# Gate weights kept in SBUF across two stages, bias tables shifted earlier, u and v stored in the order of their loads

## What is computed

```
h = rms_norm(x); proj = h @ w_in                 # u, q, k, v and two gates g
g = sigmoid(g + b_gate)
a = fourier_mix(u) @ w_fa                        # real part of a 2-D DFT, 4 groups of 128 channels
n = neighbourhood_attention(q, k, v, rpb) @ w_nb # 8 heads, 8 x 16 windows on a 32 x 64 grid
x = x + (g[0] * a + g[1] * n) @ w_out
x = x + (silu(gate) * val) @ w_down              # [val, gate] = conv3(rms_norm(x) @ w_up)
out = rms_norm(x)
```

## Time and profile before

| | us |
|---|---|
| median of 3 executions | 2981.87 |
| lowest, highest | 2978.73, 2984.8 |
| the profiled execution | 2978.5 |
| span of its trace | 2976.7 |
| PE busy in the span | 2729.0 |

### The profile page before, as it was taken

How to read it: one execution, slowest core, us unless ns; L and a number is a source line. 1 busy time by engine, 2 the same in 40 slices (tenths; PEclk the granted TensorE clock), 3 DMA queues, 4 the chain that set the end, 5 groups by cost and what they waited for, 6 DMA issues and landing times. The chain is left out here.

```text
span 2976.7 us, 33988 instructions
## 1 busy us (share of the span) xinstructions
PE 2729.0 (92%) x12792; PEld 2268.5 (76%) x12792; DVE 1406.7 (47%) x2279; ACT 886.5 (30%) x1595; POOL 871.4 (29%) x481
## 2 busy tenths in 40 slices
PE   7999999987839996899994999997999999999997
PEld 5888888866728885777783888886888888888886
DVE  5300000015328995544435999998555554122232
ACT  4311111112216662112213444443222223343332
POOL 1020011102103323433214666664000004555553
PEclk9999999998969998999996999998999999999999
DMA  4222133446477663656545777776666666554553
GB/s 146 89 96 71 61 134 136 150 169 208 152 154 178 175 172 107 198 177 177 164 134 173 276 277 275 276 281 230 233 219 220 219 221 210 174 202 138 204 174 113
DMA packets 254610, 533.03 MB, mean 179 GB/s; under 512 B 66292, under 2 KB 91632, under 8 KB 249200
## 3 DMA queue, kind: packets, MB, share of 16 engines
q1 hardware_dynamic: 231904, 507.53, 52.1%
q10 hardware_dynamic: 22544, 23.33, 2.3%
HBM read 343.03 MB, written 189.30 MB: 179 GB/s over the span
## 5 line engine op out<-in xcount | busy, mean ns | idle before, releaser
L2117 PE MATMUL ff_psum<-ff_w,ff_hid 128*128 128x512 f32 x2112 | 479.1, 389 | 0.8 <-DVE ff_hid L1834 0.8
L2117 PEld LDWEIGHTS ff_psum<-ff_w,ff_hid 128*128 128x128 f32 x2112 | 396.3, 188 | 83.4 <-issue 1.2
L1709 POOL TENSOR_TENSOR ff_w<-ff_st,ff_w 128x512 fp32r<-128x512 f32 x176 | 247.5, 1414 | 635.4 <-ACT ff_w L1953 635.3
L362 PE MATMUL in_psum<-in_hA,in_w 128*128 128x512 f32 x1728 | 393.1, 389 | 0.0
L362 PEld LDWEIGHTS in_psum<-in_hA,in_w 128*128 128x128 f32 x1728 | 324.4, 188 | 67.2
L1709 POOL TENSOR_TENSOR ff_w<-ff_wraw,ff_w 128x512 fp32r<-128x512 f32 x154 | 279.4, 1816 | 231.8 <-ACT ff_w L1953 231.7
L2078 PE MATMUL ff_psum<-ff_h,ff_w 128*128 128x512 f32 x1056 | 248.4, 395 | 40.1 <-DVE ff_h L1776 25.3
L2078 PEld LDWEIGHTS ff_psum<-ff_h,ff_w 128*128 128x128 f32 x1056 | 201.6, 191 | 83.5 <-POOL ff_w L1709 41.1
L242 DVE CAST in_w<-in_wraw 128x1024 fp32r<-128x1024 f32 x32 | 22.8, 717 | 482.9 <-PE in_psum L362 415.7
L2078 PE MATMUL ff_psum<-ff_h,ff_again 128*128 128x512 f32 x1056 | 244.8, 391 | 3.7 <-DVE ff_h L1776 3.7
L220 POOL TENSOR_TENSOR in_w<-in_wraw,in_w 128x1024 fp32r<-128x1024 f32 x32 | 77.0, 2407 | 542.1 <-DVE in_w L242 542.1
(11 more groups left out here) (174 smaller groups left out, 3887.8 us busy)
## 6 DMA issues: line engine op xcount, KB each, us to landing
split<-ff_w SPq DMA_DIRECT2D x154, 512.0 KB, 3.6
ff_again<-split SPq DMA_DIRECT2D x154, 512.0 KB, 4.1
ff_st<-in_w_down_dram SPq DMA_DIRECT2D x176, 256.0 KB, 2.9
ff_wraw<-in_w_up_dram SPq DMA_DIRECT2D x44, 512.0 KB, 5.6
hidden<-ff_c SPq DMA_DIRECT2D x44, 512.0 KB, 3.0
ff_kraw<-hidden SPq DMA_DIRECT2D x44, 512.0 KB, 4.4
at_bias<-shifted SPq DMA_DIRECT2D x72, 256.0 KB
in_wraw<-in_w_in_dram SPq DMA_DIRECT2D x32, 512.0 KB, 5.6
```

The costliest lines, as they stand in the source:

```text
L362: last = nc.tensor.matmul(ps[:, bank], w[:, a, s, k], hT(c, k, b * BLK, BLK), start=(k == 0 and (a, c) == SPLIT[0]), stop=(k == KD - 1 and ...
L1709: nc.gpsimd.tensor_tensor(split_out(i, 1), parts(i), f32(split_out(i, 0)), ALU.subtract).then_inc(w_tail, 1)
L2117: last = nc.tensor.matmul(ps[:, 4 * (1 - half) + t], hid[:, a, (b * PAIRS + pair) % 2, q, t * P:(t + 1) * P], weights(i)[:, e], start=(r = ...
```

## The change

1. Four of the six weight slots of the input stage become a tensor `keep` that outlives the stage. Gate tiles 12 to 15 are put there and are not stored; tiles 0 to 11 use the other two slots and are stored as before. The Fourier stage begins with the four kept tiles (`tile_of`), and loads the other twelve into the same four slots, each after the tile four before it.
2. The zeroing of `padded`, the copy of `rpb` and the 48 shifts move into the input stage, one shift before each of the 48 gate stores.
3. u is stored as `[group, partition, token slab, channel]`, so that a group's load is one piece of 8 KB a partition (the stores then have pieces of 512 bytes); v as `[head, 256, 8, 64]`, so that 4 DMAs with pieces of 2 KB load a head (stores: pieces of 256 bytes). The Fourier output is written over `ub`.
4. `gates`, `positions` and `channels` are put in another order on PE, and ACT's list follows; `gbias` is loaded first.
5. Attention, first head only: the tails of q and k are made in two parts, the first enough for the first row of tiles.
6. Mixer, up to weight `FIRST`: raw weights use four slots (two of them in `h2`, unused until then), and two loads are issued ahead of the first gate loads.
7. `const_in` becomes one semaphore for all stages, with raised counts.

```diff
+KEPT = 4
@@ input_phase
-        slot += [4 + t % 2 for t in range(NG)]
+        NS = NG - KEPT
+        slot += [4 + t % 2 for t in range(NS)] + [t for t in range(KEPT)]
+            def store_u(n):
+                sp.wait_ge(evac_done, n + 1)
+                sp.dma_start(u_out[:, :, n].rearrange("h b c -> b h c"),
+                             stage[:, n % STAGES].rearrange("p (h c) -> p h c", h=FNET_GROUPS)
+                             ).then_inc(stored[n % STAGES], 16)
...
-                store(n, v_out[i * P:(i + 1) * P, :])
+                rows = v_out[:, i % 2 * P:(i % 2 + 1) * P, i // 2].rearrange("h q d -> q h d")
+                sp.wait_ge(evac_done, n + 1)
+                sp.dma_start(rows, stage[:, n % STAGES].rearrange("p (h d) -> p h d", h=HEADS)
+                             ).then_inc(stored[n % STAGES], 16)
...
             for t in range(NG):
-                store_gate_w(t)
+                if t < NS:
+                    store_gate_w(t)
                 if t + 2 < NG:
                     load_gate(t + 2)
                 for b in range(GB):
+                    shift(GB * t + b)
                     store(n, gT_out[t * P:(t + 1) * P, b * BLK:(b + 1) * BLK])
@@ fourier_phase
-            def load_gate_w(t):
-                at_least(sp, gate_mm, t - GRING + 1)
-                sp.dma_start(f32(gw[:, t % GRING]), gate_w[t]).then_inc(gw_in[t % GRING], 16)
+            def load_gate_w(v):
+                sp.wait_ge(gate_mm, v - KEPT + 1)
+                sp.dma_start(f32(keep[:, :, v % KEPT]), gate_w[tile_of(v)]).then_inc(gw_in[v % KEPT], 16)
...
+            act.wait_ge(gbias_in, 16)
             gates(0, 1)
+            tables()
+            gates(2, 3)
             heads(0)
-            gates(2, 3)
+            gates(4)
             spectrum(0)
@@ attention_phase
-                for r in range(4):
-                    for j in range(TJ):
-                        sp.dma_start(vs[r * KC:(r + 1) * KC, h % 2, j::TJ],
-                                     vv[r, COL0[j]:COL0[j] + KC, :, h * HEAD_DIM:(h + 1) * HEAD_DIM]
-                                     ).then_inc(v_in[h % 2], 16)
+                for j in range(TJ):
+                    rows = v[h]
+                    src = bass.AP(rows.tensor, rows.offset + COL0[j] * run, [[GRID_W * run, 4], [run, KC], [1, run]])
+                    sp.dma_start(vs[:, h % 2, j * VG:(j + 1) * VG].rearrange("p g d -> p (g d)"), src
+                                 ).then_inc(v_in[h % 2], 16)
...
-            dve.wait_ge(qk_heads, PARTS)
-            V.tensor_tensor(kl[:, 0], kraw[:, :], f32(kh[:, 0]), ALU.subtract).then_inc(k_tail, 1)
+            first_k_tail(slice(0, KR), 2)
             masked_bias(0)
+            first_k_tail(slice(KR, ROWS), 5)
@@ mixer_output_phase
+        FIRST = mix_at[KD] + KD % 2 + 1
+        def raw_w(n):
+            if n < FIRST and n % 4 >= 2:
+                return h2[:, n % 2].rearrange("p (k q) -> p k q", q=P)
+            return wraw[:, n % 2]
...
-                at_least(sp, w_tail, n - 1)
+                at_least(sp, w_tail, n - 3 if n < FIRST else n - 1)
...
             for k in range(KA):
                 load_a(0, k)
+            load_w()
+            load_w()
             for b in range(NBLK):
```

317 lines of the change are left out of this document (166 added, 151 removed).

## The result

The changed kernel takes 2966.67 us (median of 7 executions, 2952.61 to 2976.11) where the kernel before takes 2980.5 in the same comparison. The ratio is 0.994, with a 95% interval from 0.9924 to 0.9955. So it is faster by 14 us, where 54 were forecast, and lies outside the range of 2909 to 2949. The execution that was profiled took 2959.42 us, its span is 2957.6. All medians here are of executions with a mean granted clock of 0.95 to 0.97; one execution of e1_v16 took 3184 us at 0.83, a slower state, and is left out.

A forecast was written before the change was run, and what follows sets the result against it. PE's idle times were taken as the bound, largest its waits for gate weights, then attention's DMA queue. Gains of 39.6 (Fourier), 12 (attention) and 2.5 (mixer), 54 us of 2978.5, give 2924, or 2927 as median; range 2909 to 2949.

The forecast's parts named there:

- Fourier stage, -39.6: Fourier stage: kept gate tiles and the new order end PE's idle times, a gain of 39.6 us, from 30 to 43.
- The two about cancel: Fourier stage, before positions(0): ACT makes the table's head later but the table lands earlier, so positions(0) starts at 686.5.
- The rival of the reloads: Fourier stage: reloaded gate tiles come late and become PE's wait, four waits of 5 us, 2947 us; chance 0.08.
- The rival that the kept tiles save nothing: Fourier stage: something else holds PE as long at the start, only the order's part stays, 2960 us; chance 0.04.
- Attention, -12: Attention: head 1's q and k land earlier, 11 us, and later heads give 1; gain 12 us, from 3 to 20.
- at 212 throughout: Attention's start: if the DMA queue moved all 9.5 MB at 212 GB/s, landing after 45 + 1.5 us, gain 11.
- The low last window had a DMA share of 0.76, and SP stood in it: Attention's start, kernel before: SP's list taken as the reason for the slow last window, supporting the gain of 11 us.
- attention stays bound by bytes: Attention's start: as slow as before since the queue moves the same 9.5 MB; gain 0 to 2, 2938 us; chance 0.14.
- Later heads, -1: Attention after the first head: SP's list has 10 us more slack a head, worth 1 us.
- The slower rival: Input stage: v stores hold SP or the queue so long that PE waits, 2992 us at 11 us a store; chance 0.02.
- Mixer, -2.5: Mixer start: two weight loads pass ahead of the gates, so the first weight is ready earlier; gain 2.5 us.
- I expect nothing of the ring itself: Mixer block 0: four raw-weight slots give 0, since POOL's tails and DVE's operations, excluding each other, fill a 7.3 us step.

The follow-up runs named there:

- e1_v16: The changed kernel with a head's v loaded by 16 DMAs of 32 partitions instead of 4 DMAs with 4 rows outermost: 2938.95 us, ratio 0.9855.
- e9: e1_v16 with PE's and ACT's lists in the Fourier stage in the order of the kernel before: 2956.6 us, ratio 0.9912.
- e12_before_bias16: The kernel before with only the bias tables loaded by 24 DMAs with 16 outermost instead of 8: 2978.43 us, ratio 0.9988.
- e2: e1_v16 with the bias tables loaded by 24 DMAs a head with 16 outermost instead of 8: 2930.42 us, ratio 0.9827.
- e10: e1_v16 with the 48 shifts moved back from the input stage into SP's list of the Fourier stage: 2935.23 us, ratio 0.9845.
- e3: The changed kernel with SP's mixer weight loads no longer running two ahead after block 0: 2972.45 us, ratio 0.9961.
- e5_old_v: The changed kernel with v stored and loaded as in the kernel before, 16 DMAs a head in 256-byte pieces: 2943.58 us, ratio 0.9868.
- e7_whole_tails: e1_v16 with the first head's tails of q and k made whole again, as before: 2936.45 us, ratio 0.9844.
- e6_v2: The changed kernel with a head's v loaded by 8 DMAs with 2 rows outermost: 3038.35 us, ratio 1.0185.
- e8: e1_v16 with the mixer's raw weights in two slots again and no two early loads: 2945.21 us, ratio 0.9865.
- e4: The changed kernel with the edits of e1_v16 and e3, and bias tables by 24 DMAs with 16 outermost: 2934.87 us, ratio 0.9836.

## Why the prediction was wrong, point by point

- **Fourier stage, -39.6: right.** -37.3 measured. Three terms were off by a few microseconds: PE started at 654.20 and not 652.9, since the input stage ended later; `positions(0)` was at 691.23 and not 686.5. "The two about cancel" failed there: ACT made the table's head 3.7 us later than before (671.23, not 667.53) and Y's heads at 685.26, behind the stores of two more gate tiles, so that POOL sat idle for 2.25 us before Y's tail and PE waited 7.08 us, not 3.4. And the wait at `positions(1)` was 0.65 and not 3 with its clock. The stage was 140.9 us long, 138 were forecast. The rival of the reloads fell: no wait names one. The rival that the kept tiles save nothing fell by e9: with the stage's new loads they are worth 20 us. It would have left "only the order's part" at 2960, which gives the order 7 us; that part is 18 us.
- **Attention, -12: wrong, +14.4 measured.** Two steps failed, and the runs tell them apart. A third stays open, and the sum had two slips besides.
  - The step "what changes is v: 16 DMAs of 256 pieces ... become 4 with 128 pieces of 2 KB" priced a DMA by its count and its pieces, and "at 212 throughout" took for granted that all engines carry each of them. The outermost dimension went from 32 to 4, and that costs 19.0 us in the two profiles (e1_v16), 10.6 at least, and 28 us of the medians. No row of the kernel before shows a load on 4 engines. The range had 3 us of gain as its worst end here, and should have reached below nothing. But a load on half of the engines was there to be read: with the bias tables alone the kernel before has a share of 0.53 at 198 GB/s from 920 to 924.
  - "The low last window had a DMA share of 0.76, and SP stood in it" blamed SP for the earlier trace rows. It was half of q and k, in line behind the bias tables on half the engines: with the tables on all, the share is 1.06 and the landing at 48.4 (e12_before_bias16), inside the 45 to 49 forecast. With v on all engines and the bias tables as they are, q and k of head 1 come after 56.3, a gain of 1.3 us. So the rival "attention stays bound by bytes" had the number right, 0 to 2, for the wrong reason.
  - An earlier landing was taken one to one as a shorter stage. e2 against e10 bears that out (5.9 of 6.3 us), e12 against before doesn't (3.2 of 9.2); it stays open.
  - The sum of the landing had two slips. Its 9.5 MB are of 1024 x 1024 bytes, 9.96 million bytes, so that 212 GB/s gives 47.0 + 1.5 us and a gain of 9, not 11, and 175 GB/s none (e12, at 215 GB/s, landed after 48.4). And 175 is the plain mean of two windows of which the slow one is twice as long.
- **Later heads, -1: wrong.** "SP's list has 10 us more of slack a head" does not hold: over the eight heads SP's issues of v and of the bias tables take 182 us where they took 215, 4 us a head less, since an issue of the narrow load is 2381 ns in the median where one of e1_v16 is 422. And the heads wait for the narrow load anyway: those behind the landing take 276.0 us, and 279.0 in e3, where they take 263.4 to 269.9 with v on all engines.
- **Split tails, 0: right** (e5_old_v and e7_whole_tails).
- **Input stage, 0: right for its parts.** The stores of v and u (e5_old_v) and the shifts (e10_shifts_back) cost nothing; the stage was 654.2 us, against 652.5, and between 652.8 and 654.9 in the other kernels. The slower rival had the stores as its mechanism and fell; what might have made the kernel slower was another transfer, the load of the same v, and e6_v2 shows how it would.
- **Mixer, -2.5: the mechanism was half right, +2.0 measured.** Of the 4.5 us that block 0 gained, 2.0 are the start (2.5 were forecast for it), and the rest is what "I expect nothing of the ring itself" put at nothing. "The step is full, however early the raw weight lands" failed: before, DVE waited 1.62 us in such a step for the raw weight, and with the ring it doesn't.

```profile
1201.09 1.37 DVE L1259 CAST mo_wo<-mo_wraw 128x1024 fp32r<-128x1024 f32 x1 [1.62 <-DMA mo_wraw<-in_w_out_dram]
```

```profile
1184.34 2.84 POOL L1268 TENSOR_TENSOR mo_wo<-mo_h,mo_wo 128x1024 fp32r<-128x1024 f32 x1
1184.85 2.88 DVE L1329 TENSOR_TENSOR mo_mixed<-mo_mix,mo_mixed 128x512 fp32r<-128x512 f32 x1
```

The first row is of the kernel before, the last two are of the changed kernel. These overlap, and DVE's ends 0.55 us after POOL's. The same operation took 0.68 us in the kernel before, at 1198.19, where none of POOL's ran. So a recorded length can hold the wait for the other engine, and a sum of such lengths, as the 7.3 us are, counts it twice; the step now takes 6.8. In the changed kernel's profile the gain is given back in later blocks, in which its clock is low for 10 us in two stretches where the kernel before has none. But e8 and e12, with the old ring, have such stretches too. Over all profiles the mixer takes 441.5 us in the mean of the nine kernels with the new lists, and 445.3 in the three with the old ones, so the part is worth about 4 us and the +2.0 is the scatter of two profiles.

The missing 35 us between -19.1 and -54 are 26.4 of attention, 4.5 of the mixer, 2.3 of Fourier and 1.7 of input. With v and the bias tables on all engines, e2_v16_bias16 is at 2930.42, 3 us from the forecast, but this is partly luck: its profiled execution is 48 us below that of the kernel before, where 54 were forecast, its attention has 8.1 of the 12 us, the mixer 1.2 of the 2.5, and the 3.4 us that the forecast added for the median did not come.

**Open.** Why kernels spread so differently between executions: the changed kernel and e3, both with v on 4 engines, over 24 and 17 us, e9 with v on all engines over 15, and e2, e4, e5, e7 and e10 within 7. The changed kernel and e3 have 7 and 10 executions, the others 4. Why attention differs by up to 8 us between profiles of e1, e8, e9 and e10, whose attention code is the same. And what an earlier landing is worth.

## What to carry to other kernels

When a load is rewritten into fewer DMAs with longer pieces, look at the outermost dimension of both patterns first: four DMAs with 4 outermost lost 19 us of this stage against sixteen with 32, in the same pieces. A DMA share well below 1 while engines wait for DMAs, and issues that keep SP for microseconds, are the sign of it in a profile; the count of DMAs is none. A load on half of the engines also held up the load on all engines that came behind it. And before a gain of a few microseconds is explained, look at what two profiles of the same code differ by: here up to 8 us in one stage.

## What the runs showed of the hardware

- **Width.** 2 KB pieces of the same v: attention takes 319.7 us with 32 outermost, 338.7 with 4 and 425.4 with 2. SP's median issue goes from 422 ns to 2381 and 2459. Alone in the queue, loads in 2 KB pieces with 8, 4 and 2 outermost have DMA shares of 0.53, 0.26 and 0.13 at 202, 102 and 51 GB/s.
- **A full queue isn't a faster queue.** Behind the landing, e12 has a DMA share of 0.84 where the kernel before has 0.60, at 149 and 153 GB/s. The bias tables by 24 DMAs over twice the engines keep them busy longer for the same bytes; alone they move at 149 GB/s and not at 202:

```profile
882.20:1154.90 272.70, 249.15 (x1810) 226.54 (x1810) 226.09 (x556) 165.00 (x448) 64.06 (x14) 0.93 0.84 149
```

```profile
888.20:1154.90 266.70, 244.43 (x1810) 222.30 (x1810) 225.42 (x556) 165.33 (x448) 64.08 (x14) 0.94 0.60 153
```

- **Small stores.** 16 stores of v in pieces of 256 bytes, beside 24 matmuls each, cost nothing that can be seen: 654.2 us against 654.1 for the input stage.
